# Experts in pairs of a large and a small one, tile by tile, with rows gathered and transposed in one f32 product

## The chip, the core and the metric

One core of one Trainium2 chip runs the whole kernel in one launch. The metric is the time on the device in microseconds (us), the median of repeated runs. TensorE (PE) multiplies, VectorE (DVE) and ScalarE (ACT) work elementwise and empty PSUM, GpSimd (POOL) helps a little, SyncE (SP) issues nearly all DMAs. TensorE's clock has two levels, 1.2 and 2.4 GHz; the profile gives the granted share.

## What is computed

Two decoder layers on 256 tokens of width 1024. The first is sparse attention and a dense SwiGLU, the second latent attention and a mixture of experts, which is where the change lies. Each token goes to its two best of eight experts:

```python
logits = (ht @ w_router) + b_router
top_val, top_idx = lax.top_k(logits, TOP_K)            # TOP_K = 2, N_EXPERTS = 8
gates = jax.nn.softmax(top_val, axis=-1)
combine = sum(one_hot(top_idx) * gates)                # 256 x 8
for e in range(N_EXPERTS):
    y = y + combine[:, e:e+1] * ((silu(ht @ w_gate[e]) * (ht @ w_up[e])) @ w_down[e])
```

w_gate and w_up are 1024 x 3584, w_down is 3584 x 1024, all float32: 44 MB an expert, 352 MB in all.

## The kernel before

**Precision.** A float32 weight is split into two parts of a reduced type (fp32r), w_hi and w_lo, and so are the activations. A product is then three matmuls (`product`, L1335 to 1337: hi x hi, hi x lo, lo x hi). Plain f32 matmuls and transposes are used for small things.

**The stream of weights.** All weights come in chunks of 1 MB (128 partitions x 2048 words), in one order that all engines follow. SP loads a chunk into one of RAW = 7 slots of `raw`, when TensorE has finished the chunk seven before (`mm_done`). ScalarE copies it to w_hi (`esplit`, L578; STG = 6 slots, the slot six before must be finished), VectorE subtracts to w_lo in place (`esplit`, L1142), TensorE multiplies (`echunk`). An expert has 42 chunks: 24 that hold a quarter of the rows of w_gate or w_up for two hidden blocks of 512 ("a tile" is 8 chunks: 4 of gates, then 4 of ups), 4 for the last block, and from DOWN = 28 on 14 of w_down.

**Large and small experts.** `by_size` on VectorE sorts the experts by their number of tokens and writes `order` for SP. The four larger ones (at most 128 tokens) run first, in the loop `large`; then the four smaller ones (at most 64 tokens) in `small`. A chunk of a large expert takes 12 matmuls of 512 columns (`product`). In a small one hi and lo of 64 tokens lie side by side in the 128 columns of the stationary operand, so that 8 matmuls (`both`, L1755, 1756) do; the two halves are added when the hidden block is transposed by matmuls with `fold` (`turn_small`, L1684, f32). An expert beyond these limits would take a further round (`If most > 0`), which these inputs do not enter.

**Work between the chunks.** Every engine's program is written out by hand with chunk numbers k. In a large expert ScalarE takes silu of the gates (L608), VectorE multiplies with the ups (L1202), TensorE transposes (`turn_large`, L1672), ScalarE and VectorE split the result into e_hi and e_lo (L611, L1206). `units(k, done, late)` says after which chunk which of these stands: a fixed number of chunks after the block is complete. ScalarE and VectorE are therefore held to within a few chunks of TensorE at these places. `result` writes y_hi (L597) and y_lo (L1173) of an expert's output, `bring_back` (L1654, L1655; 8 matmuls) scatters it to tokens at k = 3 of the next expert, `add_back` (L1183) adds it to X; `turn_pick` and `back` make the scattering matrix.

**The gather.** xn holds the normalized tokens. ScalarE and VectorE split it once into h_hi and h_lo (L571, L1085). For each expert `picks` makes a matrix of zeros and ones, `gather` (L1630) multiplies it with h_hi and h_lo in 8 matmuls of 512 columns, ScalarE copies the rows out to xg (L584), `turn_block` (L1639) transposes them in 8 pieces, and ScalarE and VectorE split the result into a_hi and a_lo (L590, L1168).

## Time and profile before

| | |
|---|---|
| median of 3 runs | 1457.8 us (1457.51 to 1458.13) |
| the profiled execution | 1456.4 us, span of its instructions 1454.8 us |
| TensorE, VectorE, ScalarE busy | 1348.9 (93%), 1144.6 (79%), 977.3 us (67%) |
| DMA | 422.65 MB, mean 291 GB/s |
| mixture of experts | from about 511 us to 1448 us of the span |

Busy time of TensorE is summed from matmuls that overlap, so a share near 100% says only that it had work. The chain of waits, followed back from the last instruction, gives 67% of the span to TensorE and 15% to VectorE. An average over the span hides that the large and the small experts are different stages; they are looked at apart below.

### The profile page before, as it was taken

What the parts mean: (1) busy time and instruction counts of PE and PEld (TensorE: products, weight loads), DVE (VectorE), ACT (ScalarE), POOL (GpSimd) and SP (SyncE); (2) the same over time, 40 slices, a digit from 0 to 9 for tenths busy, and PEclk for the clock granted to TensorE, in tenths of its full rate; (3) what the DMA queues carried; (4) which work ended last, traced back from release to release, by engine and by line L of the source; (5) the groups of instructions that cost most, each with busy time, mean ns of one, the idle gap of its engine ahead of it and who ended that gap; (6) DMA issues with size and microseconds to landing.
All of it is one profiled execution on the core that took longest, in us unless ns stands there. A gap on an engine that the chain in (4) does not pass through costs nothing.

```text
span 1454.8 us, 17923 instructions
## 1 busy us (share of the span) xinstructions
PE 1348.9 (93%) x6369; PEld 1088.9 (75%) x6370; DVE 1144.6 (79%) x1167; ACT 977.3 (67%) x992; POOL 39.2 (3%) x47
## 2 busy tenths in 40 slices
PE   6986999999879889999999999999999999899896
PEld 5764778888756778888888888888776677677674
DVE  4677355462685489988989888888999999999996
ACT  4546363452577377777677867677888888888884
POOL 1004000000004000000000000000000000000000
PEclk8997999999988989999999999999999999999998
DMA  8650356364350459999999999999999999999994
GB/s 311 206 173 1 118 172 197 122 231 132 110 177 1 136 200 368 367 352 356 366 343 364 362 349 356 371 365 347 406 402 410 409 403 410 410 403 409 409 402 197
DMA packets 134913, 422.65 MB, mean 291 GB/s; under 512 B 7888, under 2 KB 14790, under 8 KB 134854
## 3 DMA queue, kind: packets, MB, share of 16 engines
q1 hardware_dynamic: 133756, 419.10, 77.6%
q0 software_dynamic: 864, 2.68, 0.5%
q8 instruction: 36, 0.59, 0.2%
q14 instruction: 23, 0.19, 0.0%
q10 hardware_dynamic: 234, 0.09, 0.0%
HBM read 420.77 MB, written 1.07 MB: 290 GB/s over the span
## 4 chain that ended last, share of the span: by engine, by line
PE 67%; DVE 15%; ACT 6%; issue 6%; DMA 5%; ACTq 0%; POOL 0%; DVEq 0%; SPq 0%
PE PS L1335 18%; PE PS L1337 18%; PE PS L1336 18%; DVE w_lo L1142 8%; ACT w_hi L578 3%; PE PS L1755 2%; DMA raw<-in_w_gate_o_dram 2%; PE PS L1684 2%; PE PS L1756 2%; DMA raw<-in_w_up_o_dram 2%; DVE w_lo L707 1%; PE PS L1672 1%; PE PS L1630 1%; DMA raw<-in_w_down_o_dram 1%; PE PS L1435 1%
## 5 line engine op out<-in xcount | busy, mean ns | idle before, releaser
L1142 DVE TENSOR_TENSOR w_lo<-raw,w_hi 128x2048 fp32r<-128x2048 f32 x336 | 759.5, 2285 | 70.5 <-ACT w_hi L578 69.6
L578 ACT ACTIVATE w_hi<-raw 128x2048 fp32r<-128x2048 f32 x336 | 634.3, 1915 | 68.4 <-DMA raw<-in_w_up_o_dram 34.6
L1335 PE MATMUL PS<-w_hi,a_hi 128*128 128x512 f32 (+5 forms) x864 | 334.3, 387 | 12.3 <-DVE w_lo L707 6.6
L1337 PE MATMUL PS<-w_hi,a_lo 128*128 128x512 f32 (+5 forms) x864 | 330.6, 383 | 0.0
L1336 PE MATMUL PS<-w_lo,a_hi 128*128 128x512 f32 (+5 forms) x864 | 330.1, 382 | 0.0
L1755 PE MATMUL PS<-w_hi,a_hi 128*128 128x512 f32 x448 | 183.2, 409 | 24.5 <-DVE w_lo L1142 23.5
L1335 PEld LDWEIGHTS PS<-w_hi,a_hi 128*128 128x128 f32 x864 | 164.8, 191 | 44.4 <-issue 10.8
L1337 PEld LDWEIGHTS PS<-w_hi,a_lo 128*128 128x128 f32 x864 | 164.9, 191 | 30.8
L1336 PEld LDWEIGHTS PS<-w_lo,a_hi 128*128 128x128 f32 x864 | 164.9, 191 | 29.3
L1756 PE MATMUL PS<-w_lo,a_hi 128*128 128x512 f32 x448 | 175.6, 392 | 0.0
L707 DVE TENSOR_TENSOR w_lo<-raw,w_hi 128x2048 fp32r<-128x2048 f32 (+4 forms) x70 | 138.9, 2017 | 27.7 <-ACT w_hi L317 27.4
L1755 PEld LDWEIGHTS PS<-w_hi,a_hi 128*128 128x128 f32 x448 | 84.1, 188 | 63.2 <-DVE w_lo L1142 44.2
L317 ACT ACTIVATE w_hi<-raw 128x2048 fp32r<-128x2048 f32 (+4 forms) x70 | 114.9, 1698 | 12.6 <-PE PS L1337 12.6
L1755 PE MATMUL PS<-w_hi,e_hi 128*128 128x512 f32 x224 | 92.0, 411 | 6.0 <-DVE w_lo L1142 5.0
L1756 PEld LDWEIGHTS PS<-w_lo,a_hi 128*128 128x128 f32 x448 | 84.2, 188 | 15.7
L1335 PE MATMUL PS<-w_hi,e_hi 128*128 128x512 f32 x224 | 89.2, 398 | 0.0
L1337 PE MATMUL PS<-w_hi,e_lo 128*128 128x512 f32 x224 | 88.1, 393 | 0.0
L1756 PE MATMUL PS<-w_lo,e_hi 128*128 128x512 f32 x224 | 88.0, 393 | 0.0
L1336 PE MATMUL PS<-w_lo,e_hi 128*128 128x512 f32 x224 | 87.3, 390 | 0.0
L1755 PEld LDWEIGHTS PS<-w_hi,e_hi 128*128 128x128 f32 x224 | 42.1, 188 | 26.4 <-DVE w_lo L1142 14.8
L329 ACT ACTIVATE a_hi<-PS,gain 128x256 fp32r<-128x256 f32 x32 | 12.6, 478 | 64.6 <-PE PS L1373 62.4
L484 ACT ACTIVATE sg<-PS,nst 128x512 f32<-128x512 f32 (+1 forms) x12 | 7.2, 650 | 64.5 <-PE PS L1337 64.5
(282 smaller groups left out, 1424.0 us busy)
## 6 DMA issues: line engine op xcount, KB each, us to landing
raw<-in_w_gate_o_dram SPq DMA_DIRECT2D x112, 1024.0 KB, 5.8
raw<-in_w_up_o_dram SPq DMA_DIRECT2D x112, 1024.0 KB, 6.0
raw<-in_w_down_o_dram SPq DMA_DIRECT2D x112, 1024.0 KB, 7.3
raw<-in_w_in_e_dram SPq DMA_DIRECT2D x12, 1024.0 KB, 9.4
raw<-in_w_down_e_dram SPq DMA_DIRECT2D x11, 1024.0 KB, 5.1
raw<-in_w_gate_e_dram SPq DMA_DIRECT2D x10, 1024.0 KB, 5.1
raw<-in_w_up_e_dram SPq DMA_DIRECT2D x10, 1024.0 KB, 5.1
raw<-in_w_out_e_dram SPq DMA_DIRECT2D x4, 1024.0 KB, 5.2
```

The costliest lines, as they stand in the source:

```text
L317: nc.scalar.activation(w_hi[:, c % STG, 0:n], raw[:, c % RAW, 0:n], ACT.Copy).then_inc(hi_done, 1)
L578: nc.scalar.activation(w_hi[:, c % STG, :], raw[:, c % RAW, :], ACT.Copy).then_inc(hi_done, 1)
L707: nc.vector.tensor_tensor(w_lo[:, c % RAW, 0:n], raw[:, c % RAW, 0:n], w_hi[:, c % STG, 0:n], ALU.subtract).then_inc(lo_done, 1)
L1142: nc.vector.tensor_tensor(w_lo[:, c % RAW, :], raw[:, c % RAW, :], w_hi[:, c % STG, :], ALU.subtract).then_inc(lo_done, 1)
L1335: nc.tensor.matmul(dst, xh, wh, start=first, stop=False)
L1336: nc.tensor.matmul(dst, xh, wl, start=False, stop=False)
L1337: return nc.tensor.matmul(dst, xl, wh, start=False, stop=last)
L1435: nc.tensor.matmul(dst, v_of(h, 0), probs_t[:, h % 2, 0:S], start=True, stop=False)
L1630: ins = nc.tensor.matmul(PS[:, 4 + half, :], pick[:, t, :], part[:, t, half * NT:(half + 1) * NT], start=(t == 0 and h == 0), stop=(t == 1 ...
L1684: ins = nc.tensor.matmul(PS[:, 6 + j % 2, at:at + HALF], halves[:, j % 2, f * P:(f + 1) * P], fold[:, :], start=True, stop=True)
L1755: nc.tensor.matmul(dst, xs, wh, start=first, stop=False)
L1756: return nc.tensor.matmul(dst, xs, wl, start=False, stop=last)
```

## The change

The experts run as four pairs, the p-th largest with the p-th of the four smaller ones. The 84 chunks of a pair alternate tile by tile (`pair_chunk`): 8 chunks of the large one, 8 of the small one, three times; then 4 and 4 of the last block; then the 14 chunks of w_down of the large expert, then the 14 of the small one. All engines' programs are merged accordingly (`pair`). The small expert gets its own activations (columns P to 2P of a_hi, `es` in place of e_hi), and the large result comes from PSUM banks 2 and 3.

h_hi, h_lo, xg and `turn_block` go. `gather` multiplies xn itself (f32, stationary) by the matrix of picks (f32, moving): the rows come out selected and transposed at once, in 16 products of 128 columns for a large expert and 16 of 64 columns (`gather_small`, after chunk 1 of the pair) for a small one.

`by_size` now stands ahead of the splits of chunks 1 to 3, because SP needs the small expert's number at chunk 8; the gates' part of it becomes `combine`. The diff is cut to what is described; `large_gate`, `large_high`, `large_mul`, `large_low`, `large_body` and `small_body` are the old statements under new names, and `alone` serves the further round.

```diff
-BRING_AT, PICK_AT, GATHER_AT = 3, 16, DOWN + 5
+PAIR_CHUNKS = 2 * EXPERT_CHUNKS
+DOWN_L, DOWN_S = 2 * DOWN, 2 * DOWN + FFE // P // 2
+PICK_AT, GATHER_AT = 16, DOWN_L + 4
...
+        def large_gates(u):
+            return 16 * (u // 2) + 4 if u < FE_TILES - 1 else DOWN_L - 6
+        def large_ups(u):
+            return 16 * (u // 2) + 8 if u < FE_TILES - 1 else DOWN_L - 4
+        def small_gates(u):
+            return 16 * (u // 2) + 12 if u < FE_TILES - 1 else DOWN_L - 2
+        def small_ups(u):
+            return 16 * (u // 2) + 16 if u < FE_TILES - 1 else DOWN_L
...
+        def pair_chunk(k):
+            if k < DOWN_L - 8:
+                return k // 8 % 2 == 1, 8 * (k // 16) + k % 8
+            if k < DOWN_L:
+                return k >= DOWN_L - 4, DOWN - 4 + k % 4
+            return k >= DOWN_S, DOWN + (k - DOWN_L) % (DOWN_S - DOWN_L)
...
+            def pair_weights(p, k0, large_e, small_e):
+                for k in range(k0, PAIR_CHUNKS):
+                    small, kl = pair_chunk(k)
+                    expert_chunk(2 * p, k, small_e if small else large_e, kl)
...
-            with sp.Fori(1, NE) as p:
-                expert_weights(p, sp.value_load(order[0:1, bass.ds(p, 1)], min_val=0, max_val=NE - 1))
+            pair_weights(0, 8, 0, order_of(PAIRS))
+            with sp.Fori(1, PAIRS) as p:
+                pair_weights(p, 0, order_of(p), order_of(p + PAIRS))
 
...
-            for t in range(TT):
-                nc.scalar.activation(h_hi[:, t, :], xn[:, t, :], ACT.Copy).then_inc(sem("hnat_hi"), 1)
...
+                for k in range(ELEAD, PAIR_CHUNKS + ELEAD * follow):
+                    esplit(2 * p, k)
+                    if k == ELEAD:
+                        gathered_small(p)
+                    for j in units(k, large_gates, 2):
+                        large_gate(2 * p, p, j, large_gates(j), False)
+                    for j in units(k, large_ups, 5):
+                        large_high(p, j)
+                    for j in units(k, small_ups, 5):
+                        act.wait_ge(sem("sm_tr"), j + 1 + p * FE_TILES)
+                        if j >= 2:
...
+                        act.wait_ge(mm_done, C_MOE + small_gates(j) + p * PAIR_CHUNKS)
+                        act.wait_ge(sem("moe_tr"), j + 1 + p * FE_TILES)
+                        nc.scalar.activation(sge[:, j % 2, :], PS[:, small_gate_bank(j), :], ACT.Copy).then_inc(sem("sm_eg"), 1)
+                    for j in units(k, small_ups, 1):
+                        act.wait_ge(mm_done, C_MOE + small_ups(j) + p * PAIR_CHUNKS)
+                        nc.scalar.activation(he[:, j % 2, :], PS[:, small_up_bank(j), :], ACT.Copy).then_inc(sem("sm_ev"), 1)
+                    for j in units(k, small_ups, 7):
...
+            def combine():
                 step(nc.vector.tensor_tensor(F(1), grid(9).unsqueeze(1).to_broadcast(wide),
...
+            def small_picks(p):
+                for t in range(TT):
+                    ins = nc.vector.tensor_scalar(picks_s[:, t, :], iota[:, 0:HALF], pos[:, t, bass.ds(p + PAIRS, 1)], None,
                                                   ALU.is_equal)
...
-            def turned(i, n):
+            def gathered(n):
                 for h in range(2):
 
...
+            def gathered_small(p):
+                dve.wait_ge(sem("sm_xhi"), p + 1)
+                nc.vector.tensor_tensor(a_hi[:, :, P + HALF:2 * P], PS[:, 5, :].rearrange("p (d t) -> p d t", d=DC),
+                                        a_hi[:, :, P:P + HALF], ALU.subtract).then_inc(sem("sm_xlo"), 1)
...
+            def pair(p, follow):
+                for k in range(ELEAD, PAIR_CHUNKS + ELEAD * follow):
+                    esplit(2 * p, k)
+                    if k == ELEAD:
+                        gathered_small(p)
+                    if 6 <= k < 10:
+                        add_back(2 * p, [k - 6])
+                    for j in units(k, large_ups, 2):
+                        large_mul(2 * p, p, j, large_ups(j), False)
...
+                        nc.vector.tensor_tensor(hT[:, j % 2, :], PS[:, small_turn_bank(j), 4 * HALF:8 * HALF], sT[:, j % 2, :],
+                                                ALU.mult).then_inc(sem("sm_mul"), 1)
+                    for j in units(k, small_ups, 8):
+                        dve.wait_ge(sem("sm_hi"), j + 1 + p * FE_TILES)
...
+                        back(2 * p)
+                    if k == PICK_AT + 5:
+                        gated_picks(p + PAIRS, p + PAIRS, HALF)
+                    if follow and k == PICK_AT + 8:
+                        picks(p + 1, P)
+                    if follow and k == PICK_AT + 9:
+                        small_picks(p + 1)
+                    if follow and k == GATHER_AT + 5:
+                        gathered(p + 1)
+                    if k == DOWN_S + 3:
+                        result(2 * p, 2)
+                    if DOWN_S + 6 <= k < DOWN_S + 10:
+                        add_back(2 * p + 1, [k - DOWN_S - 6])
+                    if k == DOWN_S + 12:
+                        back(2 * p + 1)
+                    if follow and k == DOWN_S + 13:
+                        gated_picks(p + 1, p + 1, P)
+                    if follow and k == PAIR_CHUNKS + ELEAD - 1:
...
             esplit(0, 0)
-            turned(0, P)
+            gathered(0)
+            dve.wait_ge(sem("count_set"), 1)
+            by_size()
+            small_picks(0)
             for k in range(1, ELEAD):
                 esplit(0, k)
             gates()
-            by_size()
+            combine()
...
-            def gather(i):
-                pe.wait_ge(sem("moe_pick"), i + 1)
-                for half in range(2):
+            pe.wait_ge(sem("hn_set"), 4)
+            def gather(n):
+                pe.wait_ge(sem("moe_pick"), n + 1)
+                for h in range(2):
+                    for d in range(4):
+                        dc = 4 * h + d
+                        for t in range(TT):
...
+                    ins.then_inc(sem("moe_gath"), 1)
+            def gather_small(p):
+                pe.wait_ge(sem("sm_pick"), p + 1)
+                for dc in range(DC):
                     for t in range(TT):
-                        for h, part in enumerate((h_hi, h_lo)):
-                            ins = nc.tensor.matmul(PS[:, 4 + half, :], pick[:, t, :], part[:, t, half * NT:(half + 1) * NT],
-                                                   start=(t == 0 and h == 0), stop=(t == 1 and h == 1))
-                    ins.then_inc(sem("moe_gath"), 1)
...
+            def pair_waits(p, small, kl):
+                units0 = p * FE_TILES
+                if kl < DOWN - 4 and kl % 4 == 0:
+                    T, up = kl // 8, kl // 4 % 2
+                    if small:
+                        if kl == 0:
+                            pe.wait_ge(sem("sm_xlo"), p + 1)
+                        pe.wait_ge(sem("moe_mul" if up else "moe_silu"), 2 * (T + 1) + units0)
+                    elif T >= 1:
+                        pe.wait_ge(sem("sm_ev" if up else "sm_eg"), 2 * T + units0)
+                    elif not up:
+                        pe.wait_ge(sem("moe_xlo"), 2 * p + 2)
+                elif kl == DOWN - 4:
+                    if small:
+                        pe.wait_ge(sem("sm_ev"), FE_TILES - 1 + units0)
+                    else:
+                        pe.wait_ge(sem("moe_back"), 2 * p + 1)
+                elif kl == DOWN:
+                    if small:
+                        pe.wait_ge(sem("sm_ev"), FE_TILES + units0)
+                    else:
+                        pe.wait_ge(sem("sm_eg"), FE_TILES - 1 + units0)
+                if kl >= DOWN and (kl - DOWN) % 2 == 0:
+                    pe.wait_ge(sem("sm_lo" if small else "moe_alo"), (kl - DOWN) // 2 + 1 + units0)
...
+                    pair_waits(p, small, kl)
+                    if small:
+                        echunk(2 * p, k, 4 if DOWN - 4 <= kl < DOWN else 2, NT, lambda hi, lo: small_body(kl, hi, lo))
+                    else:
+                        echunk(2 * p, k, 4 if DOWN - 4 <= kl < DOWN else 2, NT, lambda hi, lo: large_body(kl, hi, lo, 2))
+                    if k == 1:
+                        gather_small(p)
+                    if k == 3:
+                        bring_back(2 * p, small=p + 1)
+                    if k == PICK_AT:
+                        pe.wait_ge(sem("moe_add"), 8 * p + 4)
+                        turn_pick(2 * p)
+                    for j in units(k, large_ups, 2):
+                        pe.wait_ge(sem("moe_mul"), j + 1 + p * FE_TILES)
+                        if j >= 2:
+                            pe.wait_ge(sem("sm_mul"), j - 1 + p * FE_TILES)
+                        else:
+                            pe.wait_ge(sem("moe_add"), 8 * p + j + 1)
+                        turn_large(j)
+                    for j in units(k, small_ups, 2):
+                        pe.wait_ge(sem("sm_ev"), j + 1 + p * FE_TILES)
+                        if j == FE_TILES - 1:
+                            pe.wait_ge(sem("sm_mul"), j + p * FE_TILES)
+                        else:
+                            pe.wait_ge(sem("moe_alo"), j + 1 + p * FE_TILES)
+                        turn_small(j)
+                    if follow and k == GATHER_AT:
+                        gather(p + 1)
+                    if k == DOWN_S + 3:
+                        pe.wait_ge(sem("sm_mul"), FE_TILES + p * FE_TILES)
+                        if follow:
+                            pe.wait_ge(sem("moe_xlo"), 2 * p + 4)
+                        bring_back(2 * p + 1)
+                    if k == DOWN_S + 8:
+                        pe.wait_ge(sem("moe_add"), 8 * p + 8)
+                        turn_pick(2 * p + 1)
```

## Rows read from the trace of the kernel before

**Rows 1.** windows, each engine's busy time, granted clock, DMA share, GB/s: large, then small experts

```profile
core 0: us, PE busy (x) PEld busy (x) DVE busy (x) ACT busy (x) POOL busy (x), PEclk, DMA share, GB/s
644.07:1012.96 368.89, 368.89 (x1675) 304.23 (x1674) 324.93 (x208) 269.01 (x188) 0.00 (x0) 1.00 0.97 358
1012.96:1441.35 428.39, 397.82 (x1880) 309.26 (x1878) 408.02 (x268) 361.62 (x293) 0.00 (x0) 1.00 1.01 398
```

**Rows 2.** DMAs of 1100 to 1430 us: gigabytes per second in 40 slices

```profile
GB/s 410 408 410 409 410 410 409 410 397 393 410 409 410 411 410 409 410 410 409 410 410 400 390 409 410 409 411 409 410 410 409 408 410 410 400 389 408 407 410 409
```

**Rows 3.** waits, total us, times, longest, 650 to 1000 us (large experts)

```profile
ACT e_hi L611 <- PE PS L1672: 38.0, 15, 4.5
...
ACT w_hi L578 <- DMA raw<-in_w_up_o_dram: 9.0, 12, 1.1
```

**Rows 4.** waits, 1030 to 1430 us (small experts)

```profile
PE PS L1755 <- DVE w_lo L1142: 27.5, 52, 0.9
ACT w_hi L578 <- DMA raw<-in_w_up_o_dram: 19.5, 40, 1.8
```

**Rows 5.** timeline (start us, length us, engine, line): ScalarE's y_hi of experts 1, 4, 8

```profile
644.07 1.12 ACT L597 ACTIVATE y_hi<-PS,st 128x1024 fp32r<-128x1024 f32 x1 [1.03 <-PE PS L1337]
...
1012.96 1.12 ACT L597 ACTIVATE y_hi<-PS,st 128x1024 fp32r<-128x1024 f32 x1 [1.00 <-PE PS L1337]
...
1441.35 1.11 ACT L597 ACTIVATE y_hi<-PS,st 128x1024 fp32r<-128x1024 f32 x1 [4.52 <-PE PS L1756]
```

**Rows 6.** timeline, two matmuls of a small expert, twelve pitches apart

```profile
1042.76 0.39 PE L1755 MATMUL PS<-w_hi,a_hi 128*128 128x512 f32 x1
...
1045.50 0.39 PE L1755 MATMUL PS<-w_hi,a_hi 128*128 128x512 f32 x1
```

**Rows 7.** chain of waits (start, length, what): the four transposes of a large expert's hidden block

```profile
675.84 0.44 PE PS L1672 x4
```

**Rows 8.** timeline, attention of layer 1: two f32 passes of 256 columns, and the next instruction

```profile
466.36 0.60 PE L1418 MATMUL PS<-qkT 96*128 96x256 f32 x2
466.79 0.49 PE L1427 MATMUL PS<-cst,lg 128*128 128x128 f32 x3
```

**Rows 9.** timeline of TensorE: a small expert's first fold matmuls and the next weight product

```profile
1036.40 1.00 PE L1684 MATMUL PS<-fold,sge 128*128 128x64 f32 x8
...
1038.11 0.48 PE L1755 MATMUL PS<-w_hi,a_hi 128*128 128x512 f32 x1
```

**Rows 10.** timeline of VectorE and ScalarE: splits of chunks; an add, the next split

```profile
1013.97 3.71 ACT L578 ACTIVATE w_hi<-raw 128x2048 fp32r<-128x2048 f32 x2
...
1016.50 6.68 DVE L1142 TENSOR_TENSOR w_lo<-raw,w_hi 128x2048 fp32r<-128x2048 f32 x3
...
1025.91 0.68 DVE L1183 TENSOR_TENSOR X<-X,PS 128x512 f32<-128x512 f32 x1
...
1026.50 2.28 DVE L1142 TENSOR_TENSOR w_lo<-raw,w_hi 128x2048 fp32r<-128x2048 f32 x1
```

**Rows 11.** timeline of TensorE and VectorE from the first gather to expert 1's fifth chunk

```profile
512.82 0.77 PE L1630 MATMUL PS<-h_hi,pick 128*128 128x512 f32 x1 [2.51 <-DVE pick L1149]
...
515.94 0.54 PE L1630 MATMUL PS<-h_lo,pick 128*128 128x512 f32 x1
...
519.33 0.51 PE L1335 MATMUL PS<-w_hi,a_hi 128*128 128x512 f32 x1 [1.50 <-DVE a_lo L1168]
...
526.52 0.17 DVE L1097 SCALAR_TENSOR_TENSOR rt<-cst,rt 128x8 f32<-128x8 f32 x1
...
529.79 0.29 DVE L1126 TENSOR_TENSOR rt<-rt 128x128 f32<-128x128 f32 x1
...
530.43 0.23 DVE L1129 TENSOR_TENSOR fold<-cst 128x64 f32<-128x64 f32 x1
530.70 0.61 DVE L1158 TENSOR_SCALAR pickg<-cst,pos,comb 128x128 f32<-128x128 f32 x2
531.21 6.70 DVE L1142 TENSOR_TENSOR w_lo<-raw,w_hi 128x2048 fp32r<-128x2048 f32 x3
```

538 lines of the change are left out of this document (223 added, 315 removed).

## The prediction

> **What bounds the kernel now.** I read three views, in this order. First the windows by stage: in the four large experts TensorE is busy for the whole of its 368.89 us while the DMAs move 358 GB/s; in the four small ones TensorE has gaps and the DMAs move 398 GB/s, close to the 410 that most slices there show [rows 1, 2]. Then the waits: with large experts ScalarE waits for TensorE's transposes (38.0 us in 350) and hardly for weights; with small ones TensorE waits for VectorE's w_lo, and ScalarE, which feeds VectorE, for the DMAs [rows 3, 4]. So a large expert is bound by TensorE (12 matmuls of 512 columns to a chunk of 1.05 MB) and a small one by the transfer (8 matmuls to the same chunk). Last the moments at which y_hi is written: a large expert takes (1012.96 - 644.07) / 3 = 122.96 us, a small one (1441.35 - 1012.96) / 4 = 107.1 us, a pair 230.1 us [rows 5]. The granted clock is 1.00, the level of 2.4 GHz, in both stages [rows 1].
>
> **TensorE's work for a pair after the change.** Twelve pitches of a weight product are 2.74 us, so one is 0.2283 us [rows 6]; a large chunk costs 2.74, a small one 1.83. Large expert: 122.96 with everything in it, less the old gather (8 products, 1.83) and its turning (8 transposes at 0.44 / 4 = 0.11, so 0.9) [rows 5, 6, 7], plus the new gather. That is 16 f32 products that the trace shows as two passes each. Two f32 passes over 256 columns take 466.79 - 466.36 = 0.43, so 128 columns cost 0.108 a pass and 32 passes 3.45 us [rows 8]. Large: 123.7. Small expert: 336 x 0.2283 = 76.7; seven pairs of folds, 1038.11 - 1036.40 = 1.71 each for 16 passes of 64 columns, 12.0 [rows 9]; bring_back 8 x 0.2283 = 1.83; turn_pick about 0.3 (two transposes); the small gather, again 32 passes of 64 columns, by the fold's 0.107 a pass [rows 9] 3.4. Small: 94.2. Together 217.9 us if TensorE never waits.
> The new gathers are the operations that the trace does not show. By columns alone [rows 8] the small one would be 1.7 us instead of 3.4; the fold has its shape, so I take 3.4. The fold pass takes 0.053 more than its columns by [rows 8]; added to the large gather's passes this makes 0.16 each and 5.1 us; I take 3.45, since [rows 8] are nearer in columns. The ends are -7 and +7 us over four pairs.
> The Trainium skill (FP8 and Floating Point Precision, TensorE Precision Notes) says that a true FP32 product takes 4 passes through the array. That would price a product of 64 columns at 256 columns, 0.11 us, and the small gather at 1.8 us; the fold row, 0.21 us for such a product, does not agree, and by the page all four small gathers together would be 6 us cheaper than in my sum.
>
> **The other resources of a pair.** Transfers: 84 chunks of 1.0486 MB at 410 GB/s are 214.8 us, at the 407 that the slices average 216.4 [rows 2]. VectorE: a split follows a split after (6.68 - 2.28) / 2 = 2.20 us and an add of 512 columns costs 0.59 [rows 10]; 84 splits are 184.8, the 43 smaller operations at most 0.59 each, 25.4, two y_lo of twice the columns at 1.2 and four picks at 0.6 [rows 11]: at most 215. ScalarE has 84 splits, 3.71 us for two, 156, and stays below [rows 10]. xg's evacuations (16 of them, ScalarE) and the split of xn into h_hi and h_lo go; they cost nothing now in the loop, as ScalarE is busy for 269 of 369 us [rows 1]; at the start I take nothing and leave 2 us for the range. So three resources lie within 2%: TensorE 217.9, transfers 216, VectorE 215. The gain is what is left of 230.1 - 217.9 = 12.2 us a pair after the phases have been smoothed, and the buffers decide that: seven raw slots, six of w_hi.
>
> **Walk through a tile pair (16 chunks).** In the large half TensorE needs 8 x 2.74 and, after chunks 16T+2 and +3, the folds of the small units before, 3.4: 25.3 us. In the small half 8 x 1.83 and two turnings of 0.44: 15.5. Transfers of eight chunks take 20.5 in either half. The large half thus banks 4.8 us, almost two chunks, and the small half spends them. VectorE cannot bank as much: its large_mul at k = 16T+10 waits until TensorE has finished chunk 16T+7, and ScalarE's sT and sge at 16T+5 to +7 hold it within three chunks. From the start of the small half VectorE must finish a split under way (1.4 left), two large_mul (1.2), the splits 11 to 16 (13.2) and one large_low (0.6) before the next large half can begin: 16.4 against 15.5, a wait of 0.9. Ends: 0 if VectorE arrives at the limit each time, 2 if a ScalarE split of 1.92 stands in front. Three tile pairs: +2.7 (0 to 6). The half tiles before the down projection are even on all three.
>
> **Walk through the down projection.** 14 large chunks (38.4, fold 1.7, gather 3.45: 43.5) leave the transfer idle, as raw can hold only seven chunks. Then 14 small chunks come, 27.8 us of TensorE with bring_back and turn_pick. VectorE starts these at most three chunks ahead, waits for y_hi (1.1) and for the split that ScalarE does behind it (1.9), and then has ten splits (22.0), four adds (2.4) and back (0.8) before TensorE's last chunk (1.8): 30.1, so 2.3 late. The transfer is no later: chunk 76, the last that has a slot, lands two transfer times after, 5.1, seven more at 2.56, then the split on ScalarE, the one on VectorE and the product, 1.9 + 2.2 + 1.8: 29. The next pair's first split follows gated_picks, 0.9 more. +3.2 (0 to 6). The added waits sm_xlo (before bring_back's fourth part and at k = 8), moe_add before turn_pick at k = 78 and moe_alo before turn_small have their producer one or more chunks earlier on VectorE, in front of a split that TensorE needs anyway; what is queued behind them on TensorE is the weight products, and I price them at nothing, at 0.6 each where VectorE has no lead. SP's order of 168 weight DMAs stays one queue; order must be known at chunk 8 instead of 42, and is written before any slot for chunk 8 is free.
> Pair: 217.9 + 2.7 + 3.2 = 223.8.
>
> **Start and end.** Before, the first gather starts at 512.82 and expert 1's first product at 519.33 [rows 11], at the low clock: eight products of 512 columns lie 3.12 / 7 = 0.45 apart, twice the pitch of [rows 6]. The new gather there is 32 passes of 0.213, 6.8 us, then copy and subtraction of the second half, 1.7: 8.5 instead of 6.5. by_size (526.52 to 529.79, and fold to 530.70: 3.5 us) and small_picks (0.6) now stand ahead of splits 1 to 3, so chunk 1 is ready 3.5 + 0.6 + 2.2 = 6.3 us after chunk 0 may start, 3.5 later than the 2.74 of the steady course; the low clock of chunk 0 lies inside that wait. The last pair gathers nothing: -3.5. From 512.82 to the last y_hi: 8.5 + 4 x 223.8 + 3.5 - 3.5 = 903.7, against 1441.35 - 512.82 = 928.5 [rows 5, 11]. That is -24.8 against the profiled execution of 1456.4; the median of the runs is 1.4 above it, so 1457.8 - 24.8 = 1433.
>
> **Rivals.**
> A, all waits hidden (VectorE and the DMAs always arrive with what they banked). For it: the averages 216 and 215 are under 217.9. Against: the limit of three chunks. 8.5 + 871.6 = 880.1, -48.4: 1409.
> B, two thirds of the gain lost: a wait of 2 us at each of the five entries into a small phase (three tiles, half tile, down), because ScalarE's evacuations, in order with its splits, wait for TensorE (such waits last up to 4.5 us now, hidden [rows 3]). P = 227.9, -8.4: 1449.
> C, slower: the same place, but the lead falls to nothing at each entry, and TensorE stands for a whole chain of ScalarE and VectorE, 1.9 + 2.3 = 4.2 us. Five of them: P = 238.9, +35.6: 1493. It decides from 12.1 / 5 = 2.4 us an entry. Against: in the large half the producers can run three chunks ahead.
> D, the change does not do what it says: raw cannot hold what the large phase banks and each half keeps its old rate, P = 230: no change. Against: 4.8 us are less than two chunks.
> E, the transfer does not keep 407 in the mixture but the 358 GB/s of the large experts, as a limit and not for want of free slots: 84 x 2.93 = 246, +64: 1522. Against: the slices at 410 in the same kernel [rows 2]. The Trainium skill (DMA: Bandwidth & Descriptors, Where 436 GB/s comes from) gives about 358 GB/s as the limit of HBM for one core, and by that rule interleaving would bring nothing. The trace does not agree: 410 held here, in a kernel on one core.
>
> **How the numbers follow.** My case 0.50, alone 1423 to 1444 (the ends of the walks and gathers); A 0.24; B 0.11; D 0.03; C 0.10; E 0.02. What a measurement can tell from no change is about 0.2%, 3 us. Faster: 0.50 + 0.24 + 0.11 = 0.85, same 0.03, slower 0.12. The range goes from A's 1409 to just past B, 1452; I leave some 0.05 below and 0.15 above.
>
> **What would show it.** In the profile after: four periods of 220 to 227 us between the y_hi of one pair and the next; DMAs near 395 GB/s (88.1 MB a pair in 224 us) with no plateau of 358 and 407; TensorE waiting for w_lo at the first large chunk of a tile pair (0.5 to 1 us) and in the small down projection (2 to 3 us a pair); gathers of 3.4 us. Wrong would be: waits above 2 us at each entry into a small half, gathers of 5 us, a DMA rate that stays under 380, or a granted clock below 1.00 inside the loop.

## The result and the profile after

The changed kernel takes 1468.8 us (median of 4 runs, 1467.1 to 1473.6) against 1457.8 us of the kernel before on the same chip: a ratio of 1.007, 95% interval 1.005 to 1.009. It is slower by 0.7%, where 1433 was forecast and 1409 to 1452 given as the range. The profiled execution took 1469.46 us, its span is 1467.6 us. Ratios here and below leave out executions far slower than the others of their kernel; there was one, 2245.4 us of the run b_unroll, with a mean granted clock of 0.55, and nothing here explains it.

The windows from one pair's first weight product to the next one's (columns as in [rows 1]), for the second pair to the last:

```profile
760.03:994.97 234.94, 225.31 (x1065) 183.54 (x1065) 212.61 (x138) 183.36 (x134) 0.00 (x0) 0.99 0.98 377
994.97:1226.77 231.80, 225.78 (x1065) 183.82 (x1065) 209.39 (x137) 180.52 (x132) 0.00 (x0) 0.99 0.98 374
1226.77:1453.15 226.38, 219.01 (x1032) 178.56 (x1032) 208.20 (x128) 175.88 (x127) 0.00 (x0) 1.00 0.97 374
```

The plateaus of 358 and 398 GB/s [rows 1] have become one rate of 374 to 377, so the change does what it says. But no pair comes near the forecast's 223.8 us: before, a pair took 230.1 [rows 5]. The last pair makes no large gather (3.5 us); with it, it would be 229.9. And the granted clock is 0.99 instead of 1.00 in two of the three: somewhere TensorE has stopped and lost its clock. The timeline at the ends of the first, second and third pair shows it (start us, length us, engine, line, idle time in brackets):

```profile
760.03 0.79 PE L1393 MATMUL PS<-w_hi,a_hi 128*128 128x512 f32 x1 [4.36 <-issue]
994.97 0.79 PE L1393 MATMUL PS<-w_hi,a_hi 128*128 128x512 f32 x1 [4.32 <-issue]
1226.77 0.47 PE L1393 MATMUL PS<-w_hi,a_hi 128*128 128x512 f32 x1 [0.69 <-DVE w_lo L1180]
```

ScalarE, same kernel and view:

```profile
769.72 1.28 ACT L615 ACT_TABLE_LOAD   x1 [6.44 <-issue]
1003.28 1.28 ACT L615 ACT_TABLE_LOAD   x1 [5.86 <-issue]
```

"issue" is time in which the engine waited for nothing that the profile shows. Waits of this size occur at the ends of pairs 1 and 2, where the loop over pairs branches back, and not at the end of pair 3, where the program runs on into the last pair's own code. The granted clock and the DMAs around the first (windows; clock, DMA share and GB/s are the last three columns):

```profile
755.00:760.00 5.00, 0.67 (x3) 0.20 (x2) 4.74 (x3) 3.00 (x2) 0.00 (x0) 0.81 1.03 408
760.00:765.00 5.00, 4.97 (x12) 3.91 (x13) 3.65 (x3) 2.91 (x2) 0.00 (x0) 0.51 1.02 404
765.00:770.00 5.00, 5.00 (x34) 4.46 (x32) 0.80 (x1) 0.28 (x1) 0.00 (x0) 1.00 0.86 295
770.00:780.00 10.00, 10.00 (x52) 8.50 (x52) 7.04 (x4) 9.96 (x8) 0.00 (x0) 1.00 0.70 247
```

TensorE stands for 4.4 us and then runs at 0.51, the level of 1.2 GHz: its first 12 products take 5.1 us instead of 2.74 [rows 6]. Together 4.4 + 2.4 = 6.8 us a branch. At the same place the DMAs fall from 408 to 247 GB/s, since a slot comes free only when TensorE has finished its chunk.

The gathers came out as forecast. A small one (32 passes of 64 columns) takes 771.37 - 767.88 = 3.49 us, a large one (128 columns) 3.48:

```profile
767.88 3.68 PE L1698 MATMUL PS<-picks_s,xn 128*128 128x64 f32 x32
771.37 0.48 PE L1393 MATMUL PS<-w_hi,a_hi 128*128 128x512 f32 x1
930.85 3.73 PE L1689 MATMUL PS<-pick,xn 128*128 128x128 f32 x32
934.33 0.48 PE L1393 MATMUL PS<-w_hi,e_hi 128*128 128x512 f32 x1
```

The waits from 740 to 1450 us (total, times, longest), which answer to [rows 3, 4]:

```profile
DVE w_lo L1180 <- ACT w_hi L615: 59.9, 73, 7.2
ACT w_hi L615 <- DMA raw<-in_w_down_o_dram: 40.6, 46, 2.0
ACT w_hi L615 <- DMA raw<-in_w_up_o_dram: 29.7, 42, 2.3
ACT w_hi L615 <- DMA raw<-in_w_gate_o_dram: 28.7, 46, 1.7
ACT L615 <- issue: 12.3, 2, 6.4
PE PS L1393 <- issue: 8.7, 2, 4.4
PE PS L1393 <- DVE w_lo L1180: 8.4, 13, 0.8
```

### The profile page after: what moved, and what is told of

Read it like the earlier page. It is cut to its first block, busy times and chain, and to the rows that moved or that the text cites. A ratio compares the mean times of both kernels' runs of the same rounds, so it can differ in the third digit from the quotient of the medians.

```text
span 1467.6 us, 18007 instructions
## 1 busy us (share of the span) xinstructions
PE 1357.1 (92%) x6497; PEld 1105.9 (75%) x6498; DVE 1143.5 (78%) x1161; ACT 974.2 (66%) x970; POOL 39.0 (3%) x47
## 4 chain that ended last, share of the span: by engine, by line
PE 63%; DVE 16%; issue 8%; DMA 7%; ACT 5%; ACTq 0%; DVEq 0%; POOL 0%; SPq 0%
PE PS L1393 18%; PE PS L1395 17%; PE PS L1394 17%; DVE w_lo L1180 9%; DMA raw<-in_w_up_o_dram 4%; PE PS L1787 3%; ACT w_hi L615 2%; DMA raw<-in_w_down_o_dram 2%; PE PS L1689 1%; DVE w_lo L746 1%; PE PS L1752 1%; PE PS L1753 1%; DMA raw<-in_w_gate_o_dram 1%; PE PS L1698 1%; PE PS L1493 1%
## 5 line engine op out<-in xcount | busy, mean ns | idle before, releaser
L1393 PE MATMUL PS<-w_hi,a_hi 128*128 128x512 f32 (+5 forms) x864 | 338.7, 392 | 33.1 <-DVE w_lo L1180 12.1
L1752 PE MATMUL PS<-w_hi,a_hi 128*128 128x512 f32 x448 | 180.0, 402 | 4.8 <-DVE w_lo L1180 4.0
L1752 PE MATMUL PS<-w_hi,es 128*128 128x512 f32 x224 | 90.2, 403 | 4.9 <-DVE w_lo L1180 4.4
L1393 PE MATMUL PS<-w_hi,e_hi 128*128 128x512 f32 x224 | 88.8, 396 | 1.6 <-DVE w_lo L1180 1.6
L1753 PE MATMUL PS<-w_lo,es 128*128 128x512 f32 x224 | 88.2, 394 | 0.0
L1394 PE MATMUL PS<-w_lo,e_hi 128*128 128x512 f32 x224 | 87.9, 392 | 0.0
L1752 PEld LDWEIGHTS PS<-w_hi,es 128*128 128x128 f32 x224 | 42.1, 188 | 20.4 <-DVE w_lo L1180 9.3
L1393 PEld LDWEIGHTS PS<-w_hi,e_hi 128*128 128x128 f32 x224 | 42.1, 188 | 13.9 <-DVE w_lo L1180 4.1
```

The lines of the kernel that those rows point to most:

```text
L1393: nc.tensor.matmul(dst, xh, wh, start=first, stop=False)
L1394: nc.tensor.matmul(dst, xh, wl, start=False, stop=False)
L1752: nc.tensor.matmul(dst, xs, wh, start=first, stop=False)
L1753: return nc.tensor.matmul(dst, xs, wl, start=False, stop=last)
```

## Experiments

Times are medians; the kernel before, run beside, had 1459.4, 1459.5, 1458.9, 1459.9 and 1460.0 us in the five groups of runs. Ratios are to it, over rounds of runs, with their 95% intervals; they can differ from the quotient of the two medians (u_late_inter: 0.9956 by the medians, 0.9938 as the ratio). Kernels with one run have none.

| kernel | us | ratio | first gather to last y_hi |
|---|---|---|---|
| before | 1457.8 | | 928.5 |
| after | 1468.8 | 1.007 (1.005 to 1.0091) | 938.8 |
| a_unroll_all | 1454.1 | 0.996 (0.9944 to 0.9976) | 922.8 |
| a_unroll_pe | 1468.2 | 1.0064 (1.0043 to 1.0084) | 934.6 |
| b_unroll | 1462.1 | 1.0014 (0.9991 to 1.0037) | 929.8 |
| b_f32 | 1463.7 | 1.0018 (1.0001 to 1.0036) | 933.5 |
| a_half_dma | 1457.0 | one run | 923.4 |
| u_half_dma | 1448.6 | one run | 917.0 |
| u_half_dve | 1428.0 | one run | 899.5 |
| u_dve_small | 1447.7 | one run | 915.1 |
| u_dve_large | 1432.1 | one run | 903.0 |
| a_raw6 | 1508.7 | one run | 978.8 |
| b_raw6 | 1466.2 | one run | 935.6 |
| u_late_mul | 1455.0 | 0.9963 (0.9947 to 0.9979) | 928.3 |
| u_late_all | 1455.2 | 0.9957 (0.9938 to 0.9976) | 921.1 |
| u_late_inter | 1452.5 | 0.9938 (0.992 to 0.9956) | 926.0 |
| u_pool_picks | 1450.3 | 0.9935 (0.9913 to 0.9957) | 921.3 |
| u_pool_all | 1452.6 | 0.9946 (0.993 to 0.9962) | 921.4 |
| u_inter_picks | 1450.5 | 0.9945 (0.9928 to 0.9961) | 921.2 |

The last column is from the profiled executions. It leaves out what lies ahead of the experts, which is nearly the same code in all of them and yet ends between 512.3 and 517.6 us: single runs are better compared by it. It scatters too: u_late_mul and u_late_all, whose medians agree within 0.2 us, differ in it by 7.3. A smaller difference between two single profiles is not clear of that scatter.

**1. The branch.** On all four engines:

```diff
-            with pe.Fori(0, PAIRS - 1) as p:
+            for p in range(PAIRS - 1):
```

> The changed kernel with the loop over pairs written out on all four engines (no branch is taken); every instruction of the work is the same. Theory 1 (what TensorE and ScalarE lose at the end of the first and of the second pair, 4.4 and about 6 us of idle time that the waits put down to nothing but issue, is the taken branch, with the weight DMAs at full rate): the two stalls go, the first two pair periods fall from 234.1 and 235.1 us to about 228, and the time falls by 12 to 14 us, to about 1456. Theory 2 (the stalls belong to the work at that place, the end of a pair, and not to the branch): the third pair's end, which has no taken branch and no stall, speaks against it, but by it the time would stay at 1468. Both expect the waits inside a pair (some 11 us a pair) to stay.

Measured 1454.1 us. The pairs, in windows as above:

```profile
753.59:982.99 229.40, 222.68 (x1065) 182.04 (x1065) 212.80 (x138) 179.98 (x131) 0.00 (x0) 1.00 1.00 386
982.99:1211.20 228.21, 222.61 (x1064) 182.05 (x1065) 212.62 (x138) 180.41 (x131) 0.00 (x0) 1.00 1.00 386
1211.20:1435.48 224.28, 218.69 (x1032) 178.46 (x1032) 208.33 (x128) 175.89 (x127) 0.00 (x0) 1.00 0.98 377
```

The stalls are gone and the clock is 1.00. From the first gather to the last y_hi it is 922.8 us instead of 938.8, 16.0 less; the ratios (1.007 and 0.996) say the same. The last pair, which no branch touches, has 2.1 of it (226.6 and 224.5 us from its first product to its y_hi). The other 13.9 lie in the stretches with the two branches, and TensorE's own stops and slow products are 2 x 6.8 = 13.6. Theory 1 holds, and with the loops written out the change gains 0.4%.

> The changed kernel with TensorE's loop over pairs alone written out; ScalarE, VectorE and SyncE keep their loops. If TensorE's own branch is what costs (its body is 2130 records of products and loads, twice that of the kernel before), nearly all of the 12 to 14 us comes back and the time is about 1456. If ScalarE's branch is as bad (it stood for 6.4 and 5.9 us ahead of a table load at the same place, and VectorE then waited 6.6 us for it), TensorE waits for w_lo instead and less than 5 us comes back: about 1465.

Measured 1468.2 us: the median is the same, and the experts' stretch is 4 us shorter instead of 16. TensorE no longer stops for its own branch, but ScalarE still does (its waits for issue add up to 14.7 us at two places), and TensorE waits for it instead, through VectorE, at bring_back:

```profile
ACT L615 <- issue: 14.7, 2, 7.5
PEld PS L1716 <- DVE a_hi L1214: 7.0, 2, 3.7
```

This is the expectation's second case. TensorE's loop written out alone is not enough. No run wrote out TensorE's and ScalarE's and left VectorE's and SP's, so whether these matter is not known.

> The kernel before with its loops over experts written out on all four engines (no branch is taken): the control for the same edit in the changed kernel. Its trace shows no stall at the ends of its loop bodies, so Theory 1 (only a long body pays at its branch) expects no change, 1457 to 1459. If writing out loops helps any kernel here, as by a few us for each of its eight bodies, it falls by 10 or more, and the changed kernel has no lead over it.

Measured 1462.1 us, no gain: the same edit is worth nothing where a loop's body is half as long (TensorE has (1675 + 1674) / 3 = 1116 records of products and weight loads in a body before [rows 1], 2130 in one after). The Trainium skill (Runtime: NRT & Kernel Launch, Instruction fetch mechanics) says that TensorE holds 2048 instructions and most engines 512, and that a taken branch to a target outside what is held has to fetch it by DMA before it goes on. Bodies of 1116 records without a stop and of 2130 with one agree with it for TensorE. For ScalarE nothing can be said, as the records leave out its waits and branches. No run here tried another length, so that the length decides is argued, not shown; that the two branches together cost 14 to 16 us is shown.

**2. The gather alone.** In the kernel before, `gather` and `turn_block` replaced by the changed kernel's products.

> The kernel before with the new gather alone: 16 f32 products of 128 columns for each expert in place of the 8 products and 8 transposes, no splitting of xn, no xg; the experts keep their order, large ones first. For a large expert, bound by TensorE, 3.45 in place of 1.83 + 0.9: +0.7 each; for a small one, where TensorE waits for VectorE, nothing; at the start +2 us, where two splits of xn by ScalarE and VectorE may give as much back. 1457.8 + 3 x 0.7 + (0 to 2) = 1458 to 1462. If the gather by itself is what made the change slower, it would show +10.

Measured 1463.7 us, a ratio of 1.0018. ScalarE's y_hi of the large experts:

```profile
773.54 1.12 ACT L594 ACTIVATE y_hi<-PS,st 128x1024 fp32r<-128x1024 f32 x1 [0.81 <-PE PS L1330]
897.23 1.12 ACT L594 ACTIVATE y_hi<-PS,st 128x1024 fp32r<-128x1024 f32 x1 [0.99 <-PE PS L1330]
```

They are 123.7 us apart, 0.7 more than before [rows 5], the forecast's difference of the gathers; from the first gather to the first y_hi it is 2.1 us longer. The gather is not what failed.

**3. Transfer or VectorE.** Half of each chunk transferred, all instructions kept in number and size: ScalarE copies the half twice into w_hi, and VectorE subtracts w_hi from itself, so all low parts of the expert weights are left out. First with the loops, then without.

```diff
-                sp.dma_start(raw[:, slot, :].rearrange(...), src)
+                sp.dma_start(raw[:, slot, 0:CW // 2].rearrange(...), src[:, 0:kh, :])
```

> The changed kernel with half of each expert chunk transferred (left out: the second half of each weight chunk and all low parts of the expert weights; the reads, splits and products keep their number and sizes). Theory A (the waits inside a pair are for the transfer, which cannot bank what the large half leaves because seven raw slots hold it back): TensorE's waits for w_lo fall to under 3 us a pair, the pair without a taken branch falls from 229.8 to about 220, and the stalls at the branches shrink too, as the buffers are full: 1468 - 4 x 9 - 6 = about 1425. Theory B (VectorE's and ScalarE's order binds: their evacuations wait for TensorE and the splits stand behind them): the waits stay, and the time stays above 1455.

> The changed kernel with all loops over pairs written out and half of each expert chunk transferred (left out: the second half of each weight chunk and all low parts of the expert weights). In the run with loops the last pair came out 2 us shorter than with whole transfers, and the waits of 0.8 to 0.9 us at the first large chunk of each tile pair were all still there. Theory B (VectorE, not the transfer, is what comes too late in a pair): 4 x 2 us less than the kernel with written-out loops, about 1446, pair periods of 226. Theory A (the transfer): periods of 219 and about 1418.

Measured 1457.0 and 1448.6 us. With the loops written out, half of the weights' traffic is worth 5.8 us of the experts' stretch, no more than the scatter; the period below is 0.9 us shorter at half the rate, and the waits of 0.8 us at the first large chunks are all there. By itself the transfer is not it.

```profile
982.88:1210.19 227.31, 222.49 (x1065) 182.05 (x1065) 211.71 (x138) 177.48 (x132) 0.00 (x0) 1.00 0.62 195
```

With the loops in, the same cut takes 15.4 us off (938.8 to 923.4), and the branches become cheaper. In a_half_dma, at the end of the first pair, with the DMAs at 171 GB/s instead of 408:

```profile
753.44 8.89 DVE L1183 TENSOR_TENSOR w_lo<-w_hi 128x2048 fp32r<-128x2048 f32 x4
758.55 0.79 PE L1396 MATMUL PS<-w_hi,a_hi 128*128 128x512 f32 x1 [3.37 <-DVE w_lo L1183]
760.41 1.28 ACT L616 ACT_TABLE_LOAD   x1 [4.08 <-issue]
```

The profile puts TensorE's wait down to w_lo, but that split is the first of the four and ended near 755.7: the stop is the branch's. TensorE's two stops are 3.4 and 2.8 us there instead of 4.4 and 4.3, ScalarE's 4.1 and 4.0 instead of 6.4 and 5.9. By these single profiles the branches cost 923.4 - 917.0 = 6.4 us in all, against 16.0 with full traffic: much of their price goes with the traffic beside them.

Next, VectorE's split cut instead. TensorE reads the half that is made twice:

```diff
-                nc.vector.tensor_tensor(w_lo[:, c % RAW, :], raw[:, c % RAW, :], w_hi[:, c % STG, :],
+                nc.vector.tensor_tensor(w_lo[:, c % RAW, 0:D], raw[:, c % RAW, 0:D], w_hi[:, c % STG, 0:D],
```

> The changed kernel with all loops over pairs written out and VectorE's split of each expert chunk over 1024 of its 2048 columns (left out: half of the low parts of the expert weights; TensorE reads the other half twice, all products, transfers and ScalarE's splits stay). Theory B (VectorE comes too late): its work of a pair falls by about 84 x 1.1 = 92 us, TensorE's waits for w_lo shrink to what the transfer alone asks for, pair periods of 219 to 221, and the time is 1420 to 1430. Theory A (the transfer): ScalarE still waits for the DMAs and TensorE for ScalarE, and the time stays above 1445.

Measured 1428.0 us, the stretch 23.3 us shorter, with every transfer in place:

```profile
971.04:1193.39 222.35, 220.49 (x1065) 182.85 (x1065) 128.19 (x137) 180.99 (x132) 0.00 (x0) 1.00 1.01 393
```

Of these 222.35 us, 5.0 are products that start late (neighbours more than 0.25 us apart, over their pitch of 0.228); the work is 217.3, where the forecast's sum had 217.9. Theory B holds so far. But which of VectorE's work? The same cut for the chunks of one expert only:

> The changed kernel with written-out loops; VectorE splits only half of each chunk of the small experts (left out: half of the low parts of their weights; everything else as before). It takes 1.1 us from 42 splits of a pair, where TensorE consumes a chunk in 1.83 us and VectorE needs 2.2. If VectorE binds by its pace in the small halves (whether or not it can store work ahead), nearly all of the 26 us that halving every split gave comes: 1428 to 1434.

> The same for the large experts alone: the same 46 us of VectorE's work of a pair are gone, but in the large halves. If VectorE's mean load is the limit (work of 213 us in 228, saved up in the large halves and spent in the small ones), this gives as much as the cut in the small halves: 1428 to 1436. If VectorE cannot store what it saves, because it can be at most five chunks ahead and comes to each small half with the same lead as now, it gives less than 8 us: 1446 to 1454.

Measured 1447.7 and 1432.1 us: the opposite of what the walk suggests. The cut in the small halves, where VectorE is hurried, gives 7.7 us of the stretch, hardly more than the scatter, the cut in the large ones 19.8. The timelines suggest why. In a_unroll_all, VectorE from the small half's third chunk to the next large chunk, whose product starts at 1069.96:

```profile
1052.53 2.28 DVE L1180 TENSOR_TENSOR w_lo<-raw,w_hi 128x2048 fp32r<-128x2048 f32 x1
1054.73 0.68 DVE L1245 TENSOR_TENSOR he<-PS,sge 128x512 f32<-128x512 f32 x1
1055.33 2.27 DVE L1180 TENSOR_TENSOR w_lo<-raw,w_hi 128x2048 fp32r<-128x2048 f32 x1
1057.53 0.68 DVE L1245 TENSOR_TENSOR he<-PS,sge 128x512 f32<-128x512 f32 x1
1058.13 8.88 DVE L1180 TENSOR_TENSOR w_lo<-raw,w_hi 128x2048 fp32r<-128x2048 f32 x4
1066.94 0.67 DVE L1250 TENSOR_TENSOR e_lo<-PS,e_hi 128x512 fp32r<-128x512 f32 x1
1067.54 2.27 DVE L1180 TENSOR_TENSOR w_lo<-raw,w_hi 128x2048 fp32r<-128x2048 f32 x1
```

Seven splits, two multiplications and a subtraction without a gap, 17.3 us. In u_dve_small the same stretch has gaps on VectorE, nearly all ended by ScalarE. ScalarE's first splits each have a gap before them, ended by a DMA:

```profile
1053.45 1.92 ACT L615 ACTIVATE w_hi<-raw 128x2048 fp32r<-128x2048 f32 x1 [0.59 <-DMA raw<-in_w_gate_o_dram]
1055.98 1.92 ACT L615 ACTIVATE w_hi<-raw 128x2048 fp32r<-128x2048 f32 x1 [0.61 <-DMA raw<-in_w_up_o_dram]
1058.50 1.92 ACT L615 ACTIVATE w_hi<-raw 128x2048 fp32r<-128x2048 f32 x1 [0.60 <-DMA raw<-in_w_up_o_dram]
```

Chunks land every 2.52 us there. From 1058.50 on ScalarE makes four splits and four copies out of PSUM almost without a gap, and the last of these splits is the one that the large chunk needs. VectorE's own row, when it splits whole chunks, is 17.3 / 7 = 2.47 us a chunk. By this reading two producers, VectorE and the transfer with ScalarE behind it, are late by nearly the same, and each hides the other: take either away (half the transfer, or VectorE's work in the small halves) and the other one ends the wait. No run took both away. What both have behind them is the split of the first large chunk itself. In u_dve_large that one takes 1.22 us instead of 2.27, and TensorE goes from the small half into the large one at its pitch of 0.23:

```profile
1012.95 0.39 PE L1761 MATMUL PS<-w_lo,a_hi 128*128 128x512 f32 x1
1013.17 0.39 PE L1394 MATMUL PS<-w_hi,a_hi 128*128 128x512 f32 x1
```

In that pair of u_dve_large no large chunk waits more than 0.3 us. In u_dve_small, with that split whole, five do, for 0.5 to 1.6 us, among them 0.92 at 1070.58. That this last link makes up all of the difference was not measured.

**4. A slot less.** RAW = 6 in both kernels.

> The changed kernel with six raw slots instead of seven. If the transfer is what the large half cannot bank, a slot less costs about one transfer (2.6 us) at each place where a large half is followed by a small one, four to five a pair, partly hidden: 20 to 40 us more, 1490 to 1510. If the producers' order binds, less than 8 us more.

> The kernel before with six raw slots instead of seven, beside the changed kernel, which lost 40 us by the same edit. The changed kernel needs the slots to carry work from the large half to the small one; the kernel before has no such halves, and its small experts run at the producers' rate anyway. By that it loses less than 15 us, below 1473. If a slot less slows every stretch that is bound by the producers, it loses as much as the changed kernel: 1495.

Measured 1508.7 and 1466.2 us; the stretch is 40.0 and 7.1 us longer. A pair of the changed kernel then takes 241 to 247 us at 360 GB/s:

```profile
1016.52:1257.96 241.44, 228.16 (x1065) 183.55 (x1065) 210.58 (x137) 181.85 (x132) 0.00 (x0) 0.99 0.95 360
```

The alternation lives on its buffers: the slot is worth about 40 us, and about 7 in the kernel before, which is within the scatter. It is the first case of the expectation: with a slot less the transfer does hold the pair back, though at seven slots halving it brought little.

**5. Ways to get the gain.** On top of the written-out loops: VectorE's `large_mul` one chunk later; then all evacuations one chunk later.

```diff
-                    for j in units(k, large_ups, 2):
+                    for j in units(k, large_ups, 3):
                         large_mul(2 * p, p, j, large_ups(j), False)
```

> The changed kernel with written-out loops and VectorE's multiplication of a large unit (large_mul) one chunk later in its order: behind the splits of chunks 16T+11 and +12 instead of +10 and +11. If the wait at the first large chunk of each tile pair comes from what VectorE does between the end of TensorE's chunk 16T+7 and that chunk, as the prediction's walk had it (one multiplication and one split in front of the eight others), it shrinks by up to 0.8 us at three to four places of a pair: 1454 - 4 x 3 = 1442. If VectorE is late by its mean rate and not by its order, the waits stay where they are: 1452 to 1456.

> As the one before, and also ScalarE's and VectorE's evacuations behind the transposes and folds (e_hi, e_lo, sT, hT, es) one chunk later. With half the transfers ScalarE waited 29 + 24 us in 670 for those transposes, with whole transfers 14 + 4. If these waits hold the producers back, a further 1 us a pair is gained: about 1438. If only VectorE's own order counts, it is the same as the one before within 2 us; and if a fold or a product then waits for what comes later, it is slower by 1 to 2 us at each of seven units of a pair: above 1460.

Measured 1455.0 and 1455.2: neither changes the time. In u_late_mul the waits at the first large chunks are still there (0.8, 0.8 and 2.0 us in its third pair): a row of work without a gap is not shortened by its order.

```diff
+DOWN_SEQ = [0, 0, 0, 1] * 4 + [0, 0, 1] + [1] * 9
```

`back` and `gated_picks` at the pair's end come four chunks later with it.

> As u_late_mul, and the down projections mixed: three chunks of the large expert and one of the small, four times, then two and one, then the nine that are left of the small. In the down projections TensorE now waits 3 to 4 us a pair in the 14 small chunks, which follow 14 large ones in which the buffers are full. If that run of 14 is the cause, 2 to 3 us a pair come back: 10 us under the kernel with the late multiplication, 1432 to 1436. If VectorE's mean rate (213 us of work in 228) is the limit, less than 3 us.

Measured 1452.5, 2.5 us under u_late_mul, with overlapping intervals, and no gain in the stretch over a_unroll_all. Then GpSimd for the one-hot tables, and for the small expert's low operand as well:

> The changed kernel with written-out loops; the one-hot tables (picks, small_picks, gated_picks, eight instructions and some 3 us of a pair) are made by GpSimd, which is idle, in place of VectorE. If VectorE's load counts, up to 3 us a pair in places come back: 1446 to 1450. If GpSimd holds up VectorE's subtractions of two SBUF operands while it works (the Trainium skill says so: SBUF, on the port pair that VectorE and GpSimd share), nothing: 1453 to 1457.

> As u_pool_picks, and the seven subtractions of a pair that make the small expert's low operand (es from hT, 256 columns each, two SBUF operands, 0.34 us on VectorE) also on GpSimd: 2.4 us of a pair less for VectorE. If its load counts, 1442 to 1448; if GpSimd holds it up, slower than u_pool_picks by 1 us for each of the 28: 1460 and more.

Measured 1450.3 and 1452.6 us. GpSimd in u_pool_all:

```profile
1049.47 2.48 POOL L1387 TENSOR_TENSOR es<-hT,es 128x256 fp32r<-128x256 f32 x1 [0.27 <-ACT es L677]
1051.93 5.33 POOL L1398 TENSOR_SCALAR pick<-cst,pos 128x128 f32<-128x128 f32 x2
```

VectorE meanwhile:

```profile
1048.90 7.39 DVE L1180 TENSOR_TENSOR w_lo<-raw,w_hi 128x2048 fp32r<-128x2048 f32 x3
```

Four splits took 8.88 us above, so three would take 6.7; beside GpSimd they take 7.39. Over the pairs, a split's mean rose from 2286 to 2312 ns, 84 x 0.026 = 2.2 us a pair. In u_pool_picks, where GpSimd makes the tables alone, it is 2288. The expectation was also wrong on the size: the tables and the subtractions are 1.7 + 2.4 us of VectorE's pair, not 3 + 2.4 (two tables of 128 columns take 0.39 together), so 1.9 is left of it. The Trainium skill (SBUF — State Buffer, SBUF: two separate sides) says that a VectorE instruction with two SBUF inputs and a GpSimd one that reads SBUF exclude each other for a whole instruction. The trace agrees. The six `pick` tables of u_pool_all (shortest, median and longest, in ns):

```profile
L1398 POOL TENSOR_SCALAR pick<-cst,pos x6: 593/2676/4759, 595.5 to 1056.7; 128x128 f32<-128x128 f32 x6
```

The longest, 4.76 us, stands beside two splits of VectorE (each reads SBUF twice), the shortest, 0.59, beside a multiplication that reads PSUM. So GpSimd waits for whole splits, while VectorE waits for the little that a GpSimd instruction takes by itself, at most 0.55 us a split (2.83 instead of 2.28), and loses about half of what it is spared (2.2 of 4.1).

> The two edits that seemed to give something together: written-out loops, the mixed down projections of u_late_inter, the one-hot tables on GpSimd as in u_pool_picks. Against the kernel before the two stood at 0.994 each, the written-out loops alone at 0.996. If the two gains are real and independent (VectorE's load and the order of the down chunks), the ratio is 0.991 to 0.992 (1446); if they are the scatter of the runs, 0.994 to 0.996.

Measured 1450.5 us, 0.9945: the scatter's case. Four kernels stand at 0.9935 to 0.9946 and within 5 us of each other in the stretch. They beat the kernel before by some 0.6%; the written-out loops alone have 0.4%, with an interval that overlaps theirs, so a gain of any edit over these is not shown.

## Why the prediction was wrong

From the first gather to the last y_hi the forecast had 903.7 us and the trace 938.8, 35.1 more.

**The branch, 16.0 us: a term that the sum did not have.** The step that failed is the one from pair to pair: the sum is four times 223.8 with nothing for the loop's branch, and the prediction gives no reason for that. The change doubled the body. What the runs show in its place is two branches at which TensorE and ScalarE stop, 13.9 us in the stretches where they lie and 2.1 in the last pair, which may be scatter. "A granted clock below 1.00 inside the loop" stood among the signs of being wrong, and it was what led to it.

**The waits inside a pair, 19.1 us: the right mechanism, under-sized.** With the loops written out: the first pair, with its start, 240.7 for 235.8 (gather to second pair), then 229.4 and 228.2 for 223.8, and 224.5 for 220.3 from the last pair's first product to its y_hi; the differences add up to 19.1. TensorE's work, 217.9 forecast, is 217.3 where it was read. The waits were priced at 2.7 + 3.2 = 5.9 us a pair; in the pair of 228.2 they are 10.3 over the forecast's work. Those of a_unroll_all from 982.99 to 1211.20:

```profile
1026.89 0.47 PE L1393 MATMUL PS<-w_hi,a_hi 128*128 128x512 f32 x1 [0.80 <-DVE w_lo L1180]
1069.96 0.47 PE L1393 MATMUL PS<-w_hi,a_hi 128*128 128x512 f32 x1 [0.75 <-DVE w_lo L1180]
1112.06 0.47 PE L1393 MATMUL PS<-w_hi,a_hi 128*128 128x512 f32 x1 [0.78 <-DVE w_lo L1180]
1135.07 0.47 PE L1393 MATMUL PS<-w_hi,e_hi 128*128 128x512 f32 x1 [0.46 <-DVE w_lo L1180]
1198.93 0.44 PE L1705 MATMUL PS<-cst,pickg 128*128 128x128 f32 x2 [1.04 <-DVE X L1229]
1208.40 0.50 PE L1752 MATMUL PS<-w_hi,es 128*128 128x512 f32 x1 [0.69 <-DVE w_lo L1180]
1211.20 0.47 PE L1393 MATMUL PS<-w_hi,a_hi 128*128 128x512 f32 x1 [0.69 <-DVE w_lo L1180]
```

- The three first large chunks of a tile pair: 0.9 each was forecast, and 0.8 of idle time stands there three times. But idle time is counted from a product's modelled end, 0.39 after its start, while the next one normally starts after 0.23, and the one behind a wait follows 0.08 late. So each costs 0.24 more than its bracket, 3.1 us in all, and 3.8 with the late small chunks ahead of the second.
- "The half tiles are even on all three" was wrong: 0.7 us, at the first chunk of the large down projection.
- The small down projection with the wrap: 3.2 forecast, 4.1 measured. Of it, 1.2 are the wait for add_back before turn_pick, which the prediction had priced at nothing, or at 0.6 without a lead.
- Some 2 us are products started 0.04 to 0.12 late, which no view counts as a wait.

The walk had VectorE's row as 16.4 us, with 1.4 of a split under way; it is 17.3, with a whole one. And it held the transfer to be "no later". As far as these runs tell, both producers are late together, and the prediction looked at them one at a time. The start was over-priced: the gather took 7.5 us for 8.5, and chunk 1 came 6.0 after chunk 0 for 6.3 (after), so the first pair's waits are larger than its 4.9 over the forecast.

**Other steps.** The gathers (3.45 and 3.4): 3.48 and 3.49, so the prices taken from the nearest rows held. By the four passes of the Trainium skill (FP8 and Floating Point Precision, TensorE Precision Notes) the small one would be an estimated 1.8 us; the trace does not agree. E, the transfer held at 358 GB/s: refuted, 377 with the loops and 393 where VectorE is fast. B asked for 2 us at each entry into a small half and C for 4.2: no such wait stands there; a_unroll_all's are at the ends of small halves and in the small down projection. D is refuted by the rates, though its time came nearer than the forecast's. The slower end came from no rival: C had the sign, by a mechanism that isn't there.

What stays open: whether the branch's price goes with the length of the body, which of VectorE and the transfer would still bind if the other were taken away in every half, and how the 19.1 us divide between them. The first gather started 1.7 us later than before (514.51), which lies within the scatter of 512.3 to 517.6.

## What to carry to other kernels

A change that lengthens a loop's body on an engine can make its branch visible: look for idle time "<- issue" at the wrap, and write the loop out on every engine, as here the one that still branched took the place of the first. Where three resources are within a few per cent, as here, an interleaving gains only what its buffers can carry, and the last link of the chain (the split of the very chunk that is waited for) can be worth more than the producer's whole load: cutting 42 us of VectorE's work of a pair gave 8 us in the small halves and 20 in the large ones, over four pairs. Before believing in one late producer, take each of them away by itself, and then both.

## What was not expected of the hardware

- A taken branch stopped TensorE for 4.4 us and ScalarE for 5.9 to 6.4 us with the DMAs at 408 GB/s; TensorE's clock was 0.51 behind it, for 12 products. With half the traffic the stops were 3.4 and 2.8 us on TensorE and 4.1 and 4.0 on ScalarE.
- A pass of an f32 product costs 0.109 us for 64 columns and for 128 alike, in the middle of fp32r work.
- Half the bytes in the same number of DMAs gave 5.8 us of 923, within the scatter, in a kernel whose DMAs are busy for 98 to 100% of the pairs.
- One GpSimd table took 0.59 us beside a VectorE instruction that reads PSUM and 4.76 beside splits, which read SBUF twice; three splits took 7.39 us instead of 6.7 beside it. VectorE makes two such tables in 0.39.
